# Token mixer of a hybrid decoder: late row root at its entry, q, k, v, z pieces as 512- and 256-column products, halves summed on GpSimd

## The chip, the core and the metric

One core of a Trainium2 chip runs the whole kernel. The metric is the device time of one execution in microseconds. An execution uses five engines that run their own instruction queues in order and meet only at semaphores: PE (TensorE, matrix products), ACT (ScalarE), DVE (VectorE), POOL (GpSimd), and SP, which here only issues the loads of weights.

## The reference

Two layers, each FFN, mixer, FFN, on 256 positions of 1024 channels in fp32:

```python
for l in range(DEPTH):                                   # DEPTH = 2
    h = rms_norm(x, ffn1_norm[l])
    x = x + 0.5 * swiglu(h, ffn1_w_gate[l], ffn1_w_up[l], ffn1_w_down[l])   # D_FF = 2816
    h = rms_norm(x, mix_norm[l])
    proj = h @ w_in[l]                                    # 1024 -> 3080 columns
    aq, ak, av, pu, dq, dk, dv, dz, db, da = jnp.split(proj, split_at, axis=-1)
    ...                                                   # rope on aq, ak
    ya = dilated_attention(aq, ak, av).reshape(B, S, ATT_WIDTH)
    yb = multiscale_pool(pu, pool_w[l], pool_scale[l])
    yc = gated_deltanet(dq, dk, dv, dz, db, da, dn_conv_w[l], ...)
    x = x + jnp.concatenate([ya, yb, yc], axis=-1) @ w_out[l]
    h = rms_norm(x, ffn2_norm[l])
    x = x + 0.5 * swiglu(h, ffn2_w_gate[l], ffn2_w_up[l], ffn2_w_down[l])
return rms_norm(x, final_norm)
```

`rms_norm` is `x * rsqrt(mean(x*x) + eps) * w`, with one root for each position (row). In `gated_deltanet`, q, k and v (4 heads of 128) go through a causal convolution of 4 taps and a silu, q and k are normalised, z goes through a silu, and b and a give the gates (a log decay and a beta for each head and position). Then comes the chunked delta rule, which needs a triangular inverse for each head.

## The kernel before

**Products in parts.** All large products are in fp32r, which keeps fewer bits than fp32. So a weight piece (128 x 1024, 512 KB) is split: ACT casts it to a high part `Wh` (L1215) and DVE subtracts to get the low part `Wl` (L1626). The input is split likewise into `Xh` and `Xl`, which lie side by side in `X`. A product is Wh·Xh + Wh·Xl + Wl·Xh. There are six slots for pieces, and SP loads the next piece into a slot when its low cast is done.

**Two forms of a piece.** `wide_piece` (L695 to 704, the FFNs') multiplies `Wh` with `Xh` and `Xl` together, 512 columns, eight times, and then `Wl` with `Xh`, 256 columns, into the right half of the bank, eight times. Somebody must then add the halves. `column_piece` (L685, the mixer's) adds all three products up in the same 256 columns, 24 products of 256 columns each, and leaves nothing to add.

**FFN.** 22 tiles of 128 hidden channels. x is turned raw on PE, and ACT and DVE scale it by the norm weight (a column) while they split it. The root of each row comes in later: PE spreads it over all partitions (L752), DVE copies it as `rB` (L1749), and POOL multiplies it in (L589, L591).

**Mixer.** Its entry is of another form. `norm` finds the roots (ACT L1293 to L1301, DVE L1645 to L1700), POOL and DVE multiply x by the norm weight, `turn_rows` (L681) turns and scales x in one product with a diagonal of roots, and `split_rows` splits it. Then come 17 pieces, i = 0 to 16: 0 to 7 are q and k of four heads, 8 holds the gates' columns, 9 to 12 are v, 13 to 16 are z. Pieces 17 on are attention, pooling and output. For each of q, k, v, ACT takes the first tap straight from the bank (L1392, `conv_first`), DVE the other three (L1809, `conv_rest`), and ACT applies silu (L1397) and, for a pair of q and k, the squares (L1403) that PE sums (L868).

The gates: DVE copies their columns (L1840), PE turns them (L861), DVE runs 16 small steps (L1844 to L1865) with an exp and a ln on ACT between. POOL forms `grow` (L611), PE sums it up over positions (L899), DVE takes differences (L1890), ACT exponentiates them. Gram products (L917), `LT` and `aT` on DVE, a select of POOL (L619, `lt_done`), and DVE's product `DT` (L1917) follow. PE turns `DT` (L930) and ACT copies it to `Dm` (L1471). From there six levels (from L985) double the inverted blocks, with the attention's pieces between.

**What sets the order.** Nothing but the code: every engine's queue is written out by hand. In the mixer ACT's queue is, for i from 0 to 7,

```python
hi_mix(layer, i + 3)
conv_first(i)
if i >= 1:
    conv_silu(i - 1)
    if i % 2 == 0:
        square(i // 2 - 1)
```

and DVE's is

```python
lo_mix(layer, i + 3)
conv_rest(i)
```

`hi_mix` waits for the slot's load and for the product that used its high part last; `lo_mix` waits for the `hi_mix` of the same piece.

## Time and profile before

| | us |
|---|---|
| median of 3 runs | 1103.63 (1102.22 to 1105.7) |
| the profiled execution, its own time | 1107.22 |
| its span in the trace | 1105.4 |
| PE busy | 1066.8 (97%) |
| DVE busy | 726.8 (66%) |
| ACT busy | 609.7 (55%) |
| POOL busy | 213.9 (19%) |

The profile is of one execution. Its span begins with the first instruction and ends with the last; 1.8 us of its time lie outside it. Products overlap in PE's pipeline and their ends are modelled, so a length of 0.39 us says little about pace; the distance of two starts does. "Idle before" names what ended an engine's wait. The mixers lie at about 207 to 371 and 746 to 910 us, the FFNs between and around them.

### The profile page before, as it was taken

The numbers are of one execution on the slowest core, as the hardware profiler recorded it, in microseconds if no ns is written. First come the engines' busy times: TensorE is split into PE (matmuls) and PEld (weight loads), VectorE is DVE, ScalarE is ACT, GpSimd is POOL, SyncE is SP. The second block draws the span as 40 slices with busy tenths as digits, with TensorE's granted clock in tenths as the row PEclk, the third lists the DMA queues.
The fourth block names the chain that finished last, engine by engine and source line by source line (L and its number), as shares of the span: only waits on it lengthen the run. The fifth ranks groups of instructions, "written<-read, shape, count | busy, mean of one in ns | idle before, by whom it ended". The sixth has DMA issues, their size and how long they took to land.

```text
span 1105.4 us, 18284 instructions
## 1 busy us (share of the span) xinstructions
PE 1066.8 (97%) x6179; PEld 929.7 (84%) x6179; DVE 726.8 (66%) x1125; ACT 609.7 (55%) x1057; POOL 213.9 (19%) x255
## 2 busy tenths in 40 slices
PE   6899999899999999999999999998999999999996
PEld 5788888798997788888878888888899878888885
DVE  4666666688437676666677666667773667666665
ACT  5555555567445655555565555556653556555554
POOL 1312112571020131211222112120002002211212
PEclk9899999999999999999999999999999999999999
DMA  6866667364321476666647666674352044766661
GB/s 198 271 186 194 189 183 216 100 168 115 119 73 39 137 240 188 195 188 185 195 133 213 190 183 196 189 202 121 100 152 96 21 152 152 210 189 184 196 191 39
DMA packets 252151, 179.27 MB, mean 162 GB/s; under 512 B 5891, under 2 KB 237576, under 8 KB 251976
## 3 DMA queue, kind: packets, MB, share of 16 engines
q1 hardware_dynamic: 251168, 176.71, 54.3%
q0 software_dynamic: 336, 1.71, 0.4%
q8 instruction: 30, 0.49, 0.2%
q10 hardware_dynamic: 600, 0.22, 0.1%
q14 instruction: 17, 0.14, 0.0%
HBM read 177.57 MB, written 1.05 MB: 162 GB/s over the span
## 4 chain that ended last, share of the span: by engine, by line
PE 87%; DVE 5%; ACT 4%; DMA 2%; issue 1%; POOL 0%; ACTq 0%; DVEq 0%; POOLq 0%; SPq 0%
PE bank L700 27%; PE bank L703 14%; PE bank L666 12%; PE bank L667 11%; PE bank L668 11%; PE bank L985 2%; PE bank L1009 2%; DMA raw<-in_ffn_w_up 1%; DVE Wl L1626 1%; ACT Wh L1215 1%; PE bank L681 1%; DVE X L1672 1%; PE bank L992 1%; ACT big L1248 1%; PE bank L917 1%
## 5 line engine op out<-in xcount | busy, mean ns | idle before, releaser
L1626 DVE TENSOR_TENSOR Wl<-raw,Wh 128x1024 fp32r<-128x1024 f32 x330 | 417.9, 1273 | 131.6 <-ACT Wh L1215 131.3
L1215 ACT ACTIVATE Wh<-raw 128x1024 fp32r<-128x1024 f32 x330 | 337.6, 1053 | 80.6 <-PE bank L668 74.7
L700 PE MATMUL bank<-X,Wh 128*128 128x512 f32 x1344 | 334.8, 391 | 0.0
L700 PEld LDWEIGHTS bank<-X,Wh 128*128 128x128 f32 x1344 | 247.0, 189 | 47.4
L589 POOL TENSOR_TENSOR gact<-gact,pooled 128x256 f32<-128x256 f32 x88 | 77.5, 880 | 606.5 <-DVE gact L1717 464.2
L703 PEld LDWEIGHTS bank<-X,Wl 128*128 128x128 f32 x1344 | 183.2, 191 | 13.8 <-DVE Wl L1626 1.0
L703 PE MATMUL bank<-X,Wl 128*128 128x256 f32 x1344 | 187.8, 283 | 0.0
L666 PE MATMUL bank<-Wh,aH 128*128 128x512 f32 x352 | 140.0, 398 | 6.4 <-DVE aL L1738 6.0
L667 PE MATMUL bank<-Wl,aH 128*128 128x512 f32 x352 | 138.9, 395 | 0.0
L668 PE MATMUL bank<-Wh,aL 128*128 128x512 f32 x352 | 137.9, 392 | 0.0
L1314 ACT ACTIVATE dec<-bank 128x256 f32<-128x256 f32 x88 | 33.6, 382 | 126.1 <-PE bank L703 125.3
L1331 ACT ACTIVATE aH<-hid 128x256 fp32r<-128x256 f32 x88 | 36.8, 418 | 92.8 <-DVE hid L1732 92.8
L666 PEld LDWEIGHTS bank<-Wh,aH 128*128 128x128 f32 x352 | 67.0, 190 | 20.1 <-issue 8.7
L591 POOL TENSOR_TENSOR gact<-gact,pooled 128x256 f32<-128x256 f32 x88 | 66.3, 754 | 80.8 <-ACT gact L1319 80.8
L666 PE MATMUL bank<-X,Wh 128*128 128x256 f32 x272 | 79.8, 294 | 1.8 <-DVE Wl L1626 1.8
L668 PEld LDWEIGHTS bank<-Wh,aL 128*128 128x128 f32 x352 | 66.7, 190 | 14.7
L1717 DVE TENSOR_TENSOR gact<-bank,dec 128x256 f32<-128x256 f32 x88 | 37.3, 424 | 61.1 <-ACT dec L1314 61.1
L668 PE MATMUL bank<-X,Wl 128*128 128x256 f32 x272 | 77.1, 283 | 0.0
L667 PE MATMUL bank<-X,Wh 128*128 128x256 f32 x272 | 77.1, 283 | 0.0
L667 PEld LDWEIGHTS bank<-Wl,aH 128*128 128x128 f32 x352 | 67.1, 191 | 10.6
L1725 DVE TENSOR_TENSOR hid<-bank,dec 128x256 f32<-128x256 f32 x88 | 37.4, 425 | 47.5 <-ACT dec L1325 47.5
L1738 DVE TENSOR_TENSOR aL<-hid,aH 128x256 fp32r<-128x256 f32 x88 | 37.4, 425 | 42.6 <-ACT aH L1331 42.6
(246 smaller groups left out, 1276.5 us busy)
## 6 DMA issues: line engine op xcount, KB each, us to landing
raw<-in_ffn_w_gate SPq DMA_DIRECT2D x88, 512.0 KB, 4.1
raw<-in_ffn_w_up SPq DMA_DIRECT2D x88, 512.0 KB, 3.7
raw<-in_ffn_w_down SPq DMA_DIRECT2D x88, 512.0 KB, 4.5
raw<-in_w_in SPq DMA_DIRECT2D x50, 512.0 KB, 3.9
raw<-in_w_out SPq DMA_DIRECT2D x16, 512.0 KB, 3.5
cst<-in_consts POOLq DMA_DIRECT2D x1, 1536.0 KB, 9.4
xr<-in_x SPq DMA_DIRECT2D x2, 512.0 KB, 4.5
norm_w<-in_mix_norm SPq DMA_DIRECT2D x2, 512.0 KB, 6.1
```

What stands on the lines that cost most here:

```text
L589: nc.gpsimd.tensor_tensor(gact[:, par, :], gact[:, par, :], rB, ALU.mult).then_inc(gate_scaled.sem, 1)
L591: nc.gpsimd.tensor_tensor(gact[:, par, :], gact[:, par, :], rB, ALU.mult).then_inc(silu_scaled.sem, 1)
L666: nc.tensor.matmul(outp, lh, rh, start=start, stop=False)
L667: nc.tensor.matmul(outp, lh, rl, start=False, stop=False)
L668: return nc.tensor.matmul(outp, ll, rh, start=False, stop=stop)
L700: nc.tensor.matmul(b[:, :], piece(Wh, s)[:, k, :], X[:, k, :, :], start=k == 0, stop=False)
L703: m = nc.tensor.matmul(b[:, SEQ:], piece(Wl, s)[:, k, :], Xh[:, k, :], start=False, stop=k == KT - 1)
L1215: return nc.scalar.activation(Wh[:, s, :], raw[:, s, :], ACT.Copy).then_inc(hi_cast.sem, 1)
L1626: return nc.vector.tensor_tensor(Wl[:, s, :], raw[:, s, :], Wh[:, s, :].bitcast(F32), ALU.subtract).then_inc(lo_cast.sem, 1)
L1717: nc.vector.tensor_tensor(gact[:, par, :], gbank[par][:, 0:SEQ], low[:, 0, par, :], ALU.add).then_inc(gsum_done.sem, 1)
L1725: nc.vector.tensor_tensor(hid[:, par, :], ubank[par][:, 0:SEQ], low[:, 1, par, :], ALU.add).then_inc(usum_done.sem, 1)
L1738: nc.vector.tensor_tensor(aL[:, par, :], hid[:, par, :], aH[:, par, :].bitcast(F32), ALU.subtract).then_inc(al_done.sem, 1)
```

## The change

The mixer's entry takes the FFNs' form (`enter`, `enter_mixer`): raw x is turned into banks 4 to 7, split with `mix_norm` as a column, and the root comes later. The first two pieces are computed in halves as the input becomes ready. For attention and pooling, ACT multiplies the root in as it copies (`scale=stat[:, c, 7:8]`); for the gates, DVE does as it copies.

The q, k, v and z pieces become wide pieces. ACT copies each whole bank (512 columns) into a ring of four places in SBUF, which lie in `PM` and `Dm`; POOL adds the halves and multiplies by `rB`; then come the taps, or z's silu, now with the ring as source. A place is free for copy i when the taps of piece i−4 are done. `PM` and `Dm` are also what the levels use. The tables for rope, which POOL computes once in layer 0, come after the second select. At the kernel's start x is turned before the norm weights, and ACT's squares come first.

```diff
+        def ring(i):
+            t, at = (PM, Dm)[i % 4 // 2], 4 * (i % 2)
+            return t[:, at:at + 4, :].rearrange("p a t -> p (a t)")
...
 # POOL
-                weigh_rows(layer, 1)
-                if layer == 0:
-                    trig_tables()
+                def scale(i):
+                    pool.wait_ge(*evacuated.at(layer, i + 1))
+                    r = ring(i)
+                    nc.gpsimd.tensor_tensor(r[:, 0:SEQ], r[:, 0:SEQ], r[:, SEQ:], ALU.add).then_inc(summed.sem, 1)
+                    pool.wait_ge(*summed.at(layer, i + 1))
+                    nc.gpsimd.tensor_tensor(r[:, 0:SEQ], r[:, 0:SEQ], rB, ALU.mult).then_inc(scaled.sem, 1)
+                pool.wait_ge(*rb_done.at(layer, 2))
+                for i in range(11):
+                    scale(i)
                 pool.wait_ge(*gstep.at(layer, 16))
                 nc.gpsimd.tensor_tensor(grow[:, :, :], tri.unsqueeze(1).broadcast_to([P, UNITS, P]),
...
+                for i in range(11, 14):
+                    scale(i)
                 for c in range(HALVES):
+                    if c == 1:
+                        scale(14)
+                        scale(15)
                     pool.wait_ge(*lt_raw.at(layer, 2 * c + 2))
...
+                if layer == 0:
+                    trig_tables()
 # PE
-                for i in range(8):
-                    split(i)
-                    column_piece(bank[i][:, 0:SEQ], MIX_SLOTS[i],
-                                 inputs_of(layer, 1) if i == 0 else None).then_inc(proj.sem, 1)
+                enter_mixer(layer)
+                for i in range(2, 8):
+                    if i == 4:
+                        pe.wait_ge(*rb_done.at(layer, 2))
+                    wide_piece(bank[i], MIX_SLOTS[i], layer, MIX_BASE + i).then_inc(proj.sem, 1)
                 split(8)
-                pe.wait_ge(*convd.at(layer, 1))
+                pe.wait_ge(*evacuated.at(layer, 1))
                 column_piece(bank[0][:, 0:SEQ], MIX_SLOTS[8]).then_inc(gates_proj.sem, 1)
                 for h in range(2):
-                    split(9 + h)
-                    pe.wait_ge(*convd.at(layer, 2 + h))
-                    column_piece(bank[1 + h][:, 0:SEQ], MIX_SLOTS[9 + h]).then_inc(proj.sem, 1)
+                    pe.wait_ge(*evacuated.at(layer, 2 + h))
+                    wide_piece(bank[1 + h], MIX_SLOTS[9 + h], layer, MIX_BASE + 9 + h).then_inc(proj.sem, 1)
                     if h == 0:
                         pe.wait_ge(*gates_copied.at(layer, 1))
...
 # ACT
+                def evacuate(i):
+                    act.wait_ge(*proj.at(layer, i + 1))
+                    if i >= 4:
+                        act.wait_ge(*convd.at(layer, i - 3))
+                    nc.scalar.activation(ring(i), pieces[i][:, :], ACT.Copy).then_inc(evacuated.sem, 1)
...
-                for i in range(8):
+                evacuate(0)
+                evacuate(1)
+                hi_mix(layer, 4)
+                conv_first(0)
+                for i in range(2, 8):
                     hi_mix(layer, i + 3)
-                    conv_first(i)
-                    if i >= 1:
-                        conv_silu(i - 1)
-                        if i % 2 == 0:
-                            square(i // 2 - 1)
+                    evacuate(i)
+                    conv_first(i - 1)
+                    conv_silu(i - 2)
+                    if i % 2 == 1:
+                        square(i // 2 - 1)
                 hi_mix(layer, 11)
+                conv_first(7)
+                conv_silu(6)
+                evacuate(8)
                 conv_silu(7)
+                square(3)
+                hi_mix(layer, 12)
                 conv_first(8)
-                hi_mix(layer, 12)
-                conv_first(9)
-                square(3)
+                evacuate(9)
...
                     if h == 1:
-                        conv_first(10)
+                        evacuate(10)
...
                 for i in (17, 18, 19):
                     hi_mix(layer, i)
+                evacuate(14)
+                evacuate(15)
                 z_silu(2)
                 z_silu(3)
                 act.preload_act_table_set(LN_EXP)
                 for c in range(HALVES):
                     act.wait_ge(*d0_turned.at(layer, c + 1))
+                    if c == 0:
+                        act.wait_ge(*z_act.at(layer, 4))
...
 # DVE
-                for i in range(8):
-                    lo_mix(layer, i + 3)
+                lo_mix(layer, 3)
+                take_root(layer, 1)
+                lo_mix(layer, 4)
+                for i in range(6):
+                    lo_mix(layer, i + 5)
                     conv_rest(i)
                 lo_mix(layer, 11)
+                conv_rest(6)
                 dve.wait_ge(*gates_proj.at(layer, 1))
-                nc.vector.tensor_copy(gate_cols, bank[0][:, 0:SEQ]).then_inc(gates_copied.sem, 1)
+                dve.wait_ge(*rb_done.at(layer, 2))
+                nc.vector.tensor_tensor(gate_cols, bank[0][:, 0:SEQ], rB, ALU.mult).then_inc(gates_copied.sem, 1)
+                conv_rest(7)
+                lo_mix(layer, 12)
                 conv_rest(8)
-                lo_mix(layer, 12)
```

How the queues stand at three places. The first pair is ACT's queue at the pieces 3 and 4 of q and k. `Wh<-raw` is a high cast, `QK<-bank` or `QK<-PM` a first tap, `QK<-QK` a silu, `early<-QK` a square. Before:

```order
L1215 ACTIVATE Wh<-raw 128x1024 [waits downs_done,landed5]
L1392 ACTIVATE QK<-bank2,prm 128x256 [waits proj]
L1397 ACTIVATE QK<-QK 128x256 [waits convd]
L1403 ACTIVATE early<-QK 128x512 [waits conv_act]
L1215 ACTIVATE Wh<-raw 128x1024 [waits proj,landed0]
```

Now, where `Dm<-bank` is the copy into the ring:

```order
L1245 ACTIVATE Wh<-raw 128x1024 [waits downs_done,landed5]
L1415 ACTIVATE Dm<-bank2 128x512 [waits proj]
L1424 ACTIVATE QK<-PM,prm 128x256 [waits scaled]
L1429 ACTIVATE QK<-QK 128x256 [waits convd]
L1245 ACTIVATE Wh<-raw 128x1024 [waits proj,landed0]
```

The cast into slot 5 (piece 5) was followed by the tap of piece 2 and the silu of piece 1; it is now followed by the copy of piece 2, the tap of piece 1 and the silu of piece 0.

The second pair is DVE's queue at the gates. `gact<-bank0` is the copy of their columns, `ga<-bank0` the first small step, `QK` and `VT` rows are taps. Before:

```order
L1626 TENSOR_TENSOR Wl<-raw,Wh 128x1024 [waits hi_cast]
L1840 COPY gact<-bank0 128x256 [waits gates_proj]
L1809 SCALAR_TENSOR_TENSOR VT<-bank1,prm,VT 128x255 [waits conv1]
L1809 SCALAR_TENSOR_TENSOR VT<-bank1,prm,VT 128x254 [waits conv_mid]
L1809 SCALAR_TENSOR_TENSOR VT<-bank1,prm,VT 128x253 [waits conv_mid]
L1626 TENSOR_TENSOR Wl<-raw,Wh 128x1024 [waits hi_cast]
L1844 COPY ga<-bank0 128x16 [waits gates_in]
```

Now:

```order
L1672 TENSOR_TENSOR Wl<-raw,Wh 128x1024 [waits hi_cast]
L1854 SCALAR_TENSOR_TENSOR QK<-Dm,prm,QK 128x255 [waits conv1]
L1854 SCALAR_TENSOR_TENSOR QK<-Dm,prm,QK 128x254 [waits conv_mid]
L1854 SCALAR_TENSOR_TENSOR QK<-Dm,prm,QK 128x253 [waits conv_mid]
L1890 TENSOR_TENSOR gact<-bank0,pooled 128x256 [waits rb_done,gates_proj]
```

The taps of piece 6 moved between the low cast of piece 11 and the gates' copy, and those of piece 7 came behind it.

The third pair is POOL's queue from `grow` to the selects in layer 0. Before:

```order
L579 TENSOR_TENSOR pooled<-pooled,qT 128x256 [waits trig_step]
L580 TENSOR_TENSOR trig<-pooled,qT 128x256 [waits trig_step]
L611 TENSOR_TENSOR grow<-cst,ga 128x1024 [waits gstep,trig_step]
L619 AFFINE_SELECT LT<-LT 128x512 [waits lt_raw] x2
L631 TENSOR_TENSOR qkr<-big,trig 128x512 [waits att_read]
```

Now (`Dm<-Dm` is a sum of halves, `Dm<-Dm,pooled` its scaling by `rB`):

```order
L615 TENSOR_TENSOR Dm<-Dm,pooled 128x256 [waits summed]
L621 TENSOR_TENSOR grow<-cst,ga 128x1024 [waits gstep]
...
L634 AFFINE_SELECT LT<-LT 128x512
L613 TENSOR_TENSOR Dm<-Dm 128x256 [waits evacuated]
L615 TENSOR_TENSOR Dm<-Dm,pooled 128x256 [waits summed]
L613 TENSOR_TENSOR Dm<-Dm 128x256 [waits evacuated]
L615 TENSOR_TENSOR Dm<-Dm,pooled 128x256 [waits summed]
L634 AFFINE_SELECT LT<-LT 128x512 [waits lt_raw]
L545 CAST pos_f<-pos_i 128x2 [waits consts_in,pos_in]
```

`grow` stands behind the scaling of the ring's copy 10, the second select behind those of copies 14 and 15 (z's third and fourth pieces), and the tables behind the select. Copies are numbered without the gates' piece: copy 8 is piece 9.

## Rows read from the trace of the kernel before

**Rows 1.** The page, part 4: shares of the chain that ended last, by engine.
```profile
PE 87%; DVE 5%; ACT 4%; DMA 2%; issue 1%; POOL 0%; ACTq 0%; DVEq 0%; POOLq 0%; SPq 0%
```

**Rows 2.** Timeline, PE: start and length in us, line, result and operands, count, [idle before].
```profile
32.72 0.77 PE L666 MATMUL bank<-Wh,aH 128*128 128x512 f32 x1 [4.43 <-DVE aL L1738]
...
201.06 0.40 PE L666 MATMUL bank<-Wh,aH 128*128 128x512 f32 x1
...
209.94 1.16 PE L681 MATMUL bank<-diag,big 128*128 128x128 f32 x8 [2.57 <-DVE diag L1700]
...
215.72 0.37 PE L666 MATMUL bank<-X,Wh 128*128 128x256 f32 x1
...
244.84 0.38 PE L861 MATMUL bank<-cst,gact 128*128 128x128 f32 x2
...
260.17 1.96 PE L899 MATMUL bank<-grow,cst 128*128 128x512 f32 x4
```

**Rows 3.** Timeline, PE, entry of the next layer's first FFN.
```profile
549.42 2.00 PE L700 MATMUL bank<-X,Wh 128*128 128x512 f32 x8
...
552.21 0.40 PE L666 MATMUL bank<-Wh,aH 128*128 128x512 f32 x1
...
567.83 2.10 PE L700 MATMUL bank<-X,Wh 128*128 128x512 f32 x8
```

**Rows 4.** Timeline, ACT, the mixer's pieces in layer 0.
```profile
220.03 1.06 ACT L1215 ACTIVATE Wh<-raw 128x1024 fp32r<-128x1024 f32 x1 [1.18 <-DVE ga L2071]
...
223.87 0.42 ACT L1397 ACTIVATE QK<-QK 128x256 f32<-128x256 f32 x1 [1.11 <-DVE QK L1809]
...
224.20 1.04 ACT L1215 ACTIVATE Wh<-raw 128x1024 fp32r<-128x1024 f32 x1
...
226.53 0.42 ACT L1397 ACTIVATE QK<-QK 128x256 f32<-128x256 f32 x1 [0.93 <-DVE QK L1809]
...
227.52 1.04 ACT L1215 ACTIVATE Wh<-raw 128x1024 fp32r<-128x1024 f32 x1
...
239.96 1.05 ACT L1215 ACTIVATE Wh<-raw 128x1024 fp32r<-128x1024 f32 x1
```

**Rows 5.** Timeline, DVE, the mixer in layer 0.
```profile
221.19 1.22 DVE L1626 TENSOR_TENSOR Wl<-raw,Wh 128x1024 fp32r<-128x1024 f32 x1 [1.20 <-ACT Wh L1215]
...
222.33 1.51 DVE L1809 SCALAR_TENSOR_TENSOR QK<-bank,prm,QK 128x255 f32<-128x255 f32 x3
...
231.81 1.22 DVE L1626 TENSOR_TENSOR Wl<-raw,Wh 128x1024 fp32r<-128x1024 f32 x1
...
243.18 0.42 DVE L1840 COPY gact<-bank 128x256 f32<-128x256 f32 x1
...
248.11 0.17 DVE L1844 COPY ga<-bank 128x16 f32<-128x16 f32 x1
...
265.20 2.16 DVE L1890 SCALAR_TENSOR_TENSOR dec<-bank,ga,cst 128x128 f32<-128x128 f32 x8
```

**Rows 6.** Timeline, POOL, the mixer in layer 0.
```profile
228.16 0.75 POOL L575 TENSOR_TENSOR pooled<-pooled,kT 128x256 f32<-128x256 f32 x1
...
232.08 1.54 POOL L575 TENSOR_TENSOR pooled<-pooled,kT 128x256 f32<-128x256 f32 x1
...
254.01 1.90 POOL L611 TENSOR_TENSOR grow<-cst,ga 128x1024 f32<-128x1024 f32 x1 [9.33 <-DVE ga L1865]
```

**Rows 7.** Timeline, ACT, ahead of the levels.
```profile
277.12 1.08 ACT L1471 ACTIVATE Dm<-bank 128x512 f32<-128x512 f32 x2
```

**Rows 8.** Timeline, PE, first products of the levels.
```profile
277.77 2.05 PE L985 MATMUL bank<-Dm,LT 128*128 128x128 f32 x16 [0.20 <-ACT Dm L1471]
```

**Rows 9.** Timeline, ACT, the kernel's start.
```profile
16.85 0.62 ACT L1248 ACTIVATE big<-xr 128x512 f32<-128x512 f32 x1
```

**Rows 10.** Busy time by stretch: PE, PEld, DVE, ACT, POOL, granted clock, DMA share, GB/s.
```profile
32.00:38.00 6.00, 5.28 (x14) 4.21 (x15) 3.87 (x6) 3.92 (x7) 2.37 (x2) 0.56 1.06 411
208.00:216.00 8.00, 5.71 (x34) 5.52 (x35) 4.90 (x12) 3.04 (x9) 7.11 (x13) 0.79 0.00 0
```

More of the change, by code:

```diff
@@ L1239, in x_ready, with inverse, norm_final, enter @@
                     act.wait_ge(*x_new.at(layer, 4 * n + quarter_no(layer, n, c, b)))
-            def enter_ffn(layer, f, cast=None):
-                n = 2 * f
+            def inverse(layer, n, c):
+                act.wait_ge(*var_done.at(layer, 2 * n + c + 1))
+                nc.scalar.activation(stat[:, c, 3:4], stat[:, c, 2:3], ACT.Ln).then_inc(ln_done.sem, 1)
+                act.wait_ge(*ln_done.at(layer, 2 * n + c + 1))
+                nc.scalar.activation(stat[:, c, 4:5], stat[:, c, 3:4], ACT.Exp, scale=-0.5).then_inc(rs_done.sem, 1)
+            def norm_final():
+                for c in range(HALVES):
+                    for b in range(2):
+                        act.wait_ge(*x_new.at(DEPTH, 2 * c + b + 1))
+                        if c == 1:
+                            act.wait_ge(*ss_done.at(DEPTH, b + 1))
+                        nc.scalar.activation(squares[b], xr[:, c, b * NW:(b + 1) * NW], ACT.Square, scale=D_MODEL ** -0.5,
+                                             accum_out=stat[:, c, b:b + 1]).then_inc(ss_done.sem, 1)
+                    inverse(DEPTH, 0, c)
+            def enter(layer, n):
+                first = layer == 0 and n == 0
                 def square(c, b):
@@ L1253, in split @@
                     if j % 4 >= 2:
-                        act.wait_ge(*xl_done.at(layer, SPLITS[n] + j - 1))
-                    nc.scalar.activation(Xh[:, k, :], xt(k), ACT.Copy,
-                                         scale=nrm_all[:, f, layer, k:k + 1]).then_inc(xh_done.sem, 1)
-                if cast is None:
-                    square(0, 0)
-                    square(1, 0)
-                act.wait_ge(*turned.at(layer, 4 * n + (2 if cast is None else 3)))
-                for j in range(4):
-                    split(j)
-                if cast is None:
+                        act.wait_ge(*xl_done.at(layer, 8 * n + j - 1))
+                    nc.scalar.activation(Xh[:, k, :], xt(n, k), ACT.Copy,
+                                         scale=nrm_all[:, n, layer, k:k + 1]).then_inc(xh_done.sem, 1)
+                square(0, 0)
+                square(1, 0)
+                if first:
                     square(0, 1)
@@ L1268, in enter_ffn @@
                         inverse(layer, n, c)
-                else:
-                    cast(0)
+                    act.wait_ge(zeroed.sem, 2)
+                act.wait_ge(*turned.at(layer, 4 * n + (3 if first else 2)))
+                for j in range(4):
+                    split(j)
+                if first:
+                    hi_first(layer, 0, 0)
+                else:
+                    square(0, 1)
+                    square(1, 1)
+                    for c in range(HALVES):
+                        inverse(layer, n, c)
                 act.wait_ge(*turned.at(layer, 4 * n + 4))
@@ L1615, in _ @@
                     hi_first(layer, 1, j)
-                enter_ffn(layer, 1)
+                enter(layer, 2)
                 ffn(layer, 1, next_casts(layer))
-            norm(DEPTH, 0)
+            norm_final()
         @block.vector
@@ L1802, in conv_rest @@
                 def conv_rest(i):
-                    src = ([bank[b] for b in range(8)] + [bank[1], bank[2], bank[7], bank[0]])[i]
+                    src = ring(i)
                     dst = QK[:, i // 2, i % 2, :] if i < 8 else VT[:, i - 8, :]
```

351 lines of the change are left out of this document (166 added, 185 removed).

## The prediction

> **What bounds the kernel now.** I read the chain that ended last first: PE holds 87% of it, with DVE and ACT at 5% and 4% [rows 1]. Then PE's timeline at the mixer's entry. The last products of the first FFN begin at 201.06; the turned and scaled input passes through L681 from 209.94, and piece 0 of the mixer begins at 215.72 [rows 2]. The chain is a row of small steps there: norms, diagonals, turning, splitting. From then on PE has no gap: its ten pieces of 24 products take 215.72 to 244.84, which is 2.91 us each (three products of 256 columns for each of eight blocks) [rows 2].
> A 512-column product with its 256-column partner costs no less: 16 of them take 549.42 to 552.21, 2.79 us [rows 3]. The means in the page's table (391 and 283 ns) are lengths of overlapping instructions and say nothing of this; starts do. So the wider products save 0.12 us a piece and no more.
> Next I read ACT's and DVE's timelines beside PE's. A cast (1.14 from its start to the next start) and three taps (1.51) take DVE 2.65 us a piece [rows 5], so DVE is nearly as full as PE, and the order of its queue and ACT's decides what happens when either gets more to do.
>
> **What the change removes.** The entry now has the form that the FFNs already have: raw x is turned, split with its norm weight, and the row's root is multiplied in later. Such an entry stands in the trace: from the last products at 552.21 to the next piece after two finished ones at 567.83 is 15.62 us [rows 3]. The old entry plus two pieces is 215.72 − 201.06 + 2 × 2.91 = 20.48 us. Gain: 4.9 us a layer. Fourteen wide pieces more give 1.7 us where PE is the bound.
>
> **What it adds, and where that lies.** Every q, k, v, z piece now goes: PE, an ACT copy of 512 columns out of its bank (0.54 us, two take 1.08 [rows 7]), a GpSimd sum, a GpSimd scaling, ACT's first tap, DVE's other taps. GpSimd's two steps take 0.75 us each when nothing disturbs them, 1.54 when DVE's cast is running [rows 6]. With four ring places, latency alone would be covered. The order is not.
> The order of ACT (first pair of ordered rows) is now cast(i+3), copy(i), first tap(i−1), silu(i−2). DVE's is cast(i+3), then taps(i−2). So silu(i−2) waits for taps that stand behind the low cast of the very piece whose high cast ACT has just made, and the next high cast stands behind that silu. Before, silu(i−1) waited for taps behind a cast from ACT's lap before, and the two engines ran side by side. Now a lap is a closed ring, and its parts are in the trace:
> – ACT cast to DVE cast: 220.03 to 221.19, 1.16 us [rows 4, 5]
> – DVE cast to first tap: 221.19 to 222.33, 1.14 [rows 5]
> – three taps to silu: 222.33 to 223.87, 1.54 [rows 4, 5]
> – silu to the next cast: 223.87 to 224.20, 0.33; with a square 226.53 to 227.52, 0.99 [rows 4]
> That is 4.17 us, or 4.83 every second lap: 27.0 us for the six laps from cast 5 to cast 11, where PE wants a piece every 2.8 us. The taps read the ring in SBUF now, not a bank; the step of 0.48 us could be 0.42 at the least, which takes 0.2 off a lap. I keep 4.5.
>
> **The timetable, on layer 0's clock.** By the FFN's entry, PE is ready for piece 2 at 201.06 + 15.62 = 216.7. From there the path to ACT's cast 5 is, as an estimate from the rows' durations: the rest of four small parameter copies 0.6, DVE's cast 3 1.14, the root's copy 0.45, GpSimd's sum and scaling of piece 0 1.6, held up by cast 4 for 1.1, and ACT's first tap 0.4. That is 222.0. Six laps: cast 11 at 248.5 to 249, against 239.96 before [rows 4]. PE waits first for piece 7 at 232, then for 8 at 237.4; the laps decide from there.
> Gates: DVE's copy of their columns stands behind cast 11 and taps 6 (second pair of ordered rows). 249.7 + 1.14 + 1.43 gives 252.2, against 243.18 [rows 5]. PE, in order, stands at their transposes from 243.6 to 252.7. Behind that wait are piece 10, to 255.9, and the sums of squares; ACT's square(3) waits for the first sum, and cast 12 stands behind it at 257.2. DVE's cast 12 and taps 8 come before the gate steps, which start at 260.9 against 248.11 [rows 5]. ACT's table switch is then hidden and the gate steps end 10.7 late.
> GpSimd: `grow` stands behind scale(10), which needs ACT's copy(10) after two inverse norms, at 266.3. So `grow` starts at 269.0 instead of 254.01 [rows 6]. PE was busy with pieces until 260.17 before [rows 2], so only 10.8 of these 15 us are seen, and the second half of the differences on DVE comes 11.0 late (one half is 1.04 of the row's 2.16 [rows 5]).
> Last, the second GpSimd select stands behind scale(14) and scale(15) (third pair). They need ACT's copies 14 and 15, which stand behind three casts, and ACT's copies into `Dm` wait for the last z silu, since `Dm` is part of the ring. By rows: copies at 285.9 and 286.5, two sums and scalings to 289.8, the select, DVE's product and PE's turn 2.3 together as an estimate, `Dm` at 292.1. The levels start at 293.2 against 277.77 [rows 8]: 15.5 us late with the gain of the entry already taken off. The levels, attention and output pieces have the same instructions as before; their scale by a column of `stat` is free. The trig tables of layer 0 move behind the select, about 35 us of GpSimd (it was through with them 9.33 before 254.01 [rows 6]); they end near 326 to 329 and the second rope is due at about 329, so I cost them nothing, with 2 us as the upper end.
>
> **The clock.** After the 4.43 us that PE waited before 32.72 [rows 2], the granted clock was 0.56 from 32 to 38, that is the 1.2 GHz level most of that time; with 2.57 us idle before 209.94 [rows 2] and small products it was 0.79 from 208 to 216 [rows 10]. The new wait before the gates' transposes is 9 us and the one before the second turn of DT about 6 us. At the low level, piece 10 and the first sum of squares take 2.7 us more on the path, and the turns and first level products 1.7 to 3 more. Both ends are kept: 15.5 a layer if the clock never falls, 21 if it falls both times. I take 18, near the upper end, since both waits are longer than the one in the row.
>
> **Kernel's start.** The squares and roots, which stood on ACT from 16.85 on [rows 9], four squares and their roots, some 3 us, move ahead of the splits into idle time; a third row of norms is loaded. Estimate: −1.5 us once (0 to −3).
>
> **Sum.** 2 × 18 − 1.5 = 34.5 us. Against the profiled execution's own 1107.2 that gives 1141.7; that execution lay 3.6 above the median of 1103.6, so for the median 1138. Own range of this case: 2 × 15 − 3 to 2 × 22, 1131 to 1148.
>
> **Rivals.**
> Faster, 5%: the ring hides everything and the entry decides. It needs ACT to run on past silu(i−2), so the taps would have to be done before ACT gets there; that holds only if DVE's cast and taps took under 1 us together, and they take 2.7. The price if it held: −2 × (4.9 + 1.7) − 1.5 gives 1089. I leave the chance for a slip of mine in reading the order.
> Partly covered, 10%: laps are as long as I say, but what follows has slack that I count as path (square(3) earlier, `grow` covered). Then about 8 us a layer: 1118.
> Lock, 10%: DVE and GpSimd hinder each other more than in the timetable. The rows show GpSimd held up by DVE's cast of two SBUF tensors (1.54 at 232.08, beside the cast at 231.81) and not by taps whose source is a bank (0.75 at 228.16) [rows 5, 6]. The new taps read two SBUF tensors. If each lap loses one GpSimd pair, 1.5 us, on DVE, six laps and two v pieces add 12 us at most a layer, half of it likely: 2 × 6 more gives 1150. The Trainium skill, "SBUF — State Buffer", section "SBUF: two separate sides", says that a DVE instruction with two SBUF inputs and a GpSimd one exclude each other, whoever starts first holding the port to its end. The cast's row agrees with that; no row here has such taps beside GpSimd. By that rule the new taps lock where the old did not, which is this rival.
> "No change" has no mechanism that I can name and lies between the first and second: 2%. The forecast itself has 73%.
>
> **Numbers.** About 0.3% of 1103.6, 3.3 us, is what a measurement of this kernel tells from no change. Faster by more: 5%. Within: 2%. Slower: 93%. Range for 8 in 10: 1118, taking in most of the second rival, to 1150.
>
> **What would show it.** ACT's high casts 5 to 11 at 4.2 and 4.8 us in turn, each silu released by DVE's taps; if they come every 2.8, the ring is not closed and I am wrong altogether. A PE wait of about 9 us before the gates' transposes, with a granted clock under 1 behind it; none means the laps are covered. `grow` behind scale(10) and the second select behind scale(15) by 10 us or more. The FFN-like entry 4.9 us shorter, whatever the total does. Taps clearly over 0.48 us, or GpSimd steps over 2 us, would speak for the lock. Spans of the FFN stages should be unchanged.

## The result, and the profile after

| | before | after |
|---|---|---|
| median of 4 runs, us | 1104.66 (1102.22 to 1106.84) | 1160.97 (1159.38 to 1165.07) |
| profiled execution, its own time | 1107.22 | 1159.72 |
| its span | 1105.4 | 1157.4 |
| PE busy | 97% | 93% |

The changed kernel takes 1.0516 of the time of the one before (95% interval 1.0478 to 1.0554): 56 us more. The forecast was 1138, with 1118 to 1150 as its range. The direction and the places were right; the size was short by 23.

The profiled spans differ by 52.0. The levels start at 303.01 instead of 277.77 [rows 8] in layer 0, 25.2 later, and at 869.25 instead of 816.75 in layer 1, 52.5 later. Counted from the last FFN piece before it (196.58 for 198.26, and 762.56 for 737.38), each mixer loses 27 us ahead of its levels, and nothing else in the program moves by as much as 2 us. PE's timeline in the first mixer of the changed kernel (start, length, line, operation, count, idle before), beside [rows 2, 8]:

```profile
196.58 2.00 PE L700 MATMUL bank<-X,Wh 128*128 128x512 f32 x8
...
214.95 2.09 PE L700 MATMUL bank<-X,Wh 128*128 128x512 f32 x8
...
231.54 2.88 PE L700 MATMUL bank<-X,Wh 128*128 128x512 f32 x8 [2.38 <-ACT Wh L1245]
...
255.54 0.69 PE L895 MATMUL bank<-cst,gact 128*128 128x128 f32 x2 [10.39 <-DVE gact L1890]
255.88 3.76 PE L700 MATMUL bank<-X,Wh 128*128 128x512 f32 x8
...
276.52 3.30 PE L931 MATMUL bank<-grow,cst 128*128 128x512 f32 x4 [1.70 <-POOL grow L621]
...
299.54 1.12 PE L961 MATMUL bank<-cst,DT 128*128 128x128 f32 x4 [4.68 <-DVE DT L1968]
...
303.01 2.60 PE L1016 MATMUL bank<-Dm,LT 128*128 128x128 f32 x16
```

The last piece of the FFN starts at 196.58, piece 2 of the mixer at 214.95, 18.4 later. Before, the same two points are at 198.26 (the row below) and 215.72 + 2 × 2.91 = 221.54 [rows 2], 23.3 apart. That is the entry's gain, 4.9, to the tenth. At the last FFN piece itself the changed kernel is 198.26 − 196.58 = 1.7 earlier; whether the new start earned that is taken up below.

```profile
198.26 2.00 PE L700 MATMUL bank<-X,Wh 128*128 128x512 f32 x8
```

The entry's 9.8 in two layers and this 1.7, 11.5 over the whole run, are then lost more than five times over. ACT's timeline, answering to [rows 4]:

```profile
219.91 1.04 ACT L1245 ACTIVATE Wh<-raw 128x1024 fp32r<-128x1024 f32 x1
...
224.52 0.42 ACT L1429 ACTIVATE QK<-QK 128x256 f32<-128x256 f32 x1 [2.69 <-DVE QK L1854]
224.84 1.05 ACT L1245 ACTIVATE Wh<-raw 128x1024 fp32r<-128x1024 f32 x1
...
230.44 1.04 ACT L1245 ACTIVATE Wh<-raw 128x1024 fp32r<-128x1024 f32 x1
...
251.42 1.04 ACT L1245 ACTIVATE Wh<-raw 128x1024 fp32r<-128x1024 f32 x1
...
261.75 0.63 ACT L1435 ACTIVATE early<-QK 128x512 f32<-128x512 f32 x1 [4.03 <-PE bank L902]
```

The `Wh<-raw` rows are casts 5, 6, 7 and 11: laps of 4.93 and 5.60, and 31.5 us for six of them. Each silu waits 2.7 for DVE's taps: the ring is closed, as forecast, but each lap is 0.76 longer than the forecast's 4.17 and 4.83. DVE and POOL show where that is, first DVE (beside [rows 5]), then POOL (beside [rows 6]):

```profile
225.93 1.23 DVE L1672 TENSOR_TENSOR Wl<-raw,Wh 128x1024 fp32r<-128x1024 f32 x1 [1.44 <-ACT Wh L1245]
227.07 2.36 DVE L1854 SCALAR_TENSOR_TENSOR QK<-PM,prm,QK 128x255 f32<-128x255 f32 x3
...
253.64 1.51 DVE L1854 SCALAR_TENSOR_TENSOR QK<-Dm,prm,QK 128x255 f32<-128x255 f32 x3
```

```profile
226.45 1.29 POOL L613 TENSOR_TENSOR Dm<-Dm 128x256 f32<-128x256 f32 x1 [2.76 <-ACT Dm L1415]
227.82 0.81 POOL L615 TENSOR_TENSOR Dm<-Dm,pooled 128x256 f32<-128x256 f32 x1
...
274.39 2.08 POOL L621 TENSOR_TENSOR grow<-cst,ga 128x1024 f32<-128x1024 f32 x1
...
298.12 0.64 POOL L634 TENSOR_SCALAR_AFFINE_SELECT LT<-LT 128x512 f32<-128x512 f32 x1
```

Three taps take 2.36 where POOL's sum and scaling lie beside them (226.45 to 228.6), and 1.51 at 253.64, where POOL rests. The sum takes 1.29 instead of 0.75. Grouped by shape, the taps of 255 columns on the ring's half in `PM` (216 to 262 us; line, operation, operands, count, busy time, mean ns, idle before) take 958 ns on average, the one that meets GpSimd's sum:

```profile
L1854 DVE SCALAR_TENSOR_TENSOR QK<-PM,prm,QK 128x255 f32<-128x255 f32 x4 | 3.8, 958 | 0.0
```

The lock (DVE and GpSimd holding each other up) was a rival with 10% in the forecast, but it does not replace the ring: it is there in each of the six laps, on top of the ring. This is the rest of the mixer, by what PE waited for over the whole run (total, times, longest):

```profile
PE bank L895 <- DVE gact L1890: 19.7, 2, 10.4
PE bank L961 <- DVE DT L1968: 11.7, 4, 4.7
PE bank L700 <- ACT Wh L1245: 6.0, 3, 2.4
...
PE bank L931 <- POOL grow L621: 3.4, 2, 1.7
PE bank L700 <- ACT early L1440: 3.1, 2, 1.6
```

And the clock behind the 10.4 us wait (stretch, length, PE, PEld, DVE, ACT, POOL busy, granted clock, DMA share, GB/s):

```profile
245.00:262.00 17.00, 6.61 (x24) 4.97 (x23) 8.50 (x13) 6.20 (x12) 3.68 (x4) 0.70 0.21 59
```

Piece 10 takes 4.75, from 255.88 to the first sum of squares at 260.63, where a wide piece takes 2.79 at the full clock [rows 3].

### The profile page after: what moved, and what is told of

Its sections match the earlier page's. It is cut to its first block, busy times and chain, and to the rows that moved or that the text cites. A ratio compares the mean times of both kernels' runs of the same rounds, so it can differ in the third digit from the quotient of the medians.

```text
span 1157.4 us, 17864 instructions
## 1 busy us (share of the span) xinstructions
PE 1079.1 (93%) x5899; PEld 923.1 (80%) x5899; DVE 745.5 (64%) x1137; ACT 630.7 (54%) x1097; POOL 266.4 (23%) x313
## 4 chain that ended last, share of the span: by engine, by line
PE 77%; DVE 12%; ACT 6%; issue 2%; POOL 1%; DMA 1%; SPq 0%; DVEq 0%; ACTq 0%; POOLq 0%
PE bank L700 27%; PE bank L703 14%; PE bank L684 9%; PE bank L685 9%; PE bank L686 9%; DVE Wl L1672 3%; ACT Wh L1245 2%; DVE QK L1854 2%; PE bank L1016 2%; PE bank L1040 2%; DVE VT L1854 1%; DVE X L1716 1%; ACT X L1303 1%; PE bank L745 1%; DVE xr L1843 1%
## 5 line engine op out<-in xcount | busy, mean ns | idle before, releaser
L700 PE MATMUL bank<-X,Wh 128*128 128x512 f32 x1568 | 400.0, 398 | 9.2 <-ACT Wh L1245 6.0
L700 PEld LDWEIGHTS bank<-X,Wh 128*128 128x128 f32 x1568 | 291.1, 191 | 71.2 <-ACT Wh L1245 5.2
L703 PEld LDWEIGHTS bank<-X,Wl 128*128 128x128 f32 x1568 | 215.3, 192 | 17.6 <-DVE Wl L1672 2.3
L703 PE MATMUL bank<-X,Wl 128*128 128x256 f32 x1568 | 220.7, 284 | 0.1
L685 PEld LDWEIGHTS bank<-Wl,aH 128*128 128x128 f32 x352 | 66.4, 189 | 10.4
L684 PE MATMUL bank<-Wh,X 128*128 128x384 f32 (+2 forms) x160 | 57.4, 358 | 0.0
L686 PE MATMUL bank<-Wh,X 128*128 128x384 f32 (+2 forms) x160 | 55.5, 347 | 0.0
L685 PE MATMUL bank<-Wl,X 128*128 128x384 f32 (+2 forms) x160 | 55.4, 346 | 0.0
```

The lines of the kernel that those rows point to most:

```text
L684: nc.tensor.matmul(outp, lh, rh, start=start, stop=False)
L685: nc.tensor.matmul(outp, lh, rl, start=False, stop=False)
L686: return nc.tensor.matmul(outp, ll, rh, start=False, stop=stop)
L700: nc.tensor.matmul(b[:, :], piece(Wh, s)[:, k, :], X[:, k, :, :], start=k == 0, stop=False)
L703: m = nc.tensor.matmul(b[:, SEQ:], piece(Wl, s)[:, k, :], Xh[:, k, :], start=False, stop=k == KT - 1)
```

## The experiments

Three theories were on the table. The forecast's is an order that closes ACT and DVE into one lap. The rival's is the lock. A third is that what follows the gates is late for reasons of its own. Each run's ratio is to the kernel before in the same series, whose median was 1103.5 to 1105.2.

**GpSimd's work made tiny.**

```diff
-                    nc.gpsimd.tensor_tensor(r[:, 0:SEQ], r[:, 0:SEQ], r[:, SEQ:], ALU.add).then_inc(summed.sem, 1)
+                    nc.gpsimd.tensor_tensor(r[:, 0:8], r[:, 0:8], r[:, SEQ:SEQ + 8], ALU.add).then_inc(summed.sem, 1)
...
-                    nc.gpsimd.tensor_tensor(r[:, 0:SEQ], r[:, 0:SEQ], rB, ALU.mult).then_inc(scaled.sem, 1)
+                    nc.gpsimd.tensor_tensor(r[:, 0:8], r[:, 0:8], rB[:, 0:8], ALU.mult).then_inc(scaled.sem, 1)
```

> GpSimd's sum and scaling of each ring place are done over 8 columns instead of 256 (so most of the sum and of the root is left out of the output); order and semaphores are those of the changed kernel. Theory (lock): the three taps take 2.36 us beside GpSimd's work and 1.51 where it rests, because DVE and GpSimd wait for each other. Then all taps fall to about 1.5, laps from 4.93 and 5.58 to about 4.2 and 4.8, 0.75 times six per layer in the ring, and with the v taps and the k norms (0.42 against 0.96 and more) about 6 to 8 us a layer: 1161 to about 1147. Rival (reading SBUF costs the taps this much by themselves): taps stay at 2.36, laps within 0.1, time 1155 to 1161.

Measured 1132.57 (1130.74 to 1135.35), 28.4 less than the changed kernel, ratio to before 1.0271 (1.0239 to 1.0303). DVE's taps and ACT's casts 5, 6, 7 in its timeline:

```profile
224.35 1.52 DVE L1854 SCALAR_TENSOR_TENSOR QK<-PM,prm,QK 128x255 f32<-128x255 f32 x3
```

```profile
218.04 1.04 ACT L1245 ACTIVATE Wh<-raw 128x1024 fp32r<-128x1024 f32 x1
...
222.13 1.04 ACT L1245 ACTIVATE Wh<-raw 128x1024 fp32r<-128x1024 f32 x1
...
226.88 1.05 ACT L1245 ACTIVATE Wh<-raw 128x1024 fp32r<-128x1024 f32 x1
```

The same taps on the same SBUF ring take 1.52, so reading SBUF costs nothing by itself: GpSimd beside them does. The lock shows from the other side too: a sum over 8 columns takes 0.20 where DVE leaves it alone (217.11) and 0.75 beside the taps (223.74). Laps are 4.09 and 4.75, and the forecast's ring (4.17, 4.83) is met within 0.1. But the time fell by 14 a layer and not by 6 to 8.

Its levels start at 288.33 against 303.01, 14.7 earlier, from the same start (last FFN piece at 196.64 and 196.58). The two traces show where this comes from. Cast 5 is 1.9 earlier (218.04 against 219.91), because the first piece's sum and scaling are short. The six laps give 5.0 more. From cast 11 to DVE's copy ahead of the differences (274.09 against 285.47) it is 4.5, and in this stretch DVE goes through the taps of v and the norms: taps of 2.35 take 1.52 and norm steps of 0.96 take 0.41, while `grow` keeps its length (2.08 and 2.07). The sums and scalings of the last two z places, which stand ahead of the second select, take 0.9 instead of 3.0, 2.1 less. The last 1.3 come between that select and the levels, where PE ran at a granted 0.50 (299 to 303) in the changed kernel and at 0.81 (285 to 289) here. So the lock is 5.0 + 4.5 = 9.5 of the 14.7 in layer 0, and most of the rest is GpSimd's own shorter work, 1.9 and 2.1, and the clock, 1.3.

**The ring opened.**

```diff
                     conv_first(i - 1)
-                    conv_silu(i - 2)
-                    if i % 2 == 1:
-                        square(i // 2 - 1)
+                    if i >= 3:
+                        conv_silu(i - 3)
+                    if i >= 4 and i % 2 == 0:
+                        square(i // 2 - 2)
...
                 conv_first(7)
+                conv_silu(5)
+                square(2)
+                evacuate(8)
                 conv_silu(6)
-                evacuate(8)
```

> ACT's silu of q and k pieces is one lap later (silu of i-3 behind the copy of i), so that it waits for taps of DVE's lap before; all else as in the changed kernel. Theory (closed lap): laps fall from 4.93 and 5.58 to DVE's own work, a cast 1.14 and locked taps 2.36, 3.5 us; cast 11 comes about 10 us earlier in each layer, PE's wait for the gates falls from 10.4 to 3 or less, and 6 to 9 us a layer are left at the levels: 1161 to about 1145. Rival (the two engines are simply full, or the lock alone makes the laps): laps stay over 4.5 and the time within 4 us of 1161.

Measured 1140.56 (1139.53 to 1140.74), 20.4 less, ratio to before 1.0332 (1.0302 to 1.0362). Cast 5 is at 223.14 and cast 11 at 242.27 in its trace: 19.1 for six laps instead of 31.5. PE's wait for the gates is 6.7, not the 3 that was expected, since DVE with locked taps (up to 2.73) is now the slow engine itself.

**The gates' copy earlier.**

```diff
                 for i in range(6):
+                    if i == 5:
...
+                        nc.vector.tensor_tensor(gate_cols, bank[0][:, 0:SEQ], rB,
+                                                ALU.mult).then_inc(gates_copied.sem, 1)
                     lo_mix(layer, i + 5)
                     conv_rest(i)
                 lo_mix(layer, 11)
                 conv_rest(6)
...
-                nc.vector.tensor_tensor(gate_cols, bank[0][:, 0:SEQ], rB, ALU.mult).then_inc(gates_copied.sem, 1)
```

> DVE copies the gates' columns ahead of the low cast of piece 10 instead of behind that of piece 11 and taps 6; all else as in the changed kernel. Theory (place in the queue): PE's wait before the gates' transposes falls from 10.4 us to under 2, piece 10 and the sums of squares run at the full clock, ACT's square(3) no longer waits 4.0 us; 4 to 6 us a layer earlier at the levels: about 1151. Rival (what follows hangs on ACT's laps and not on this wait): PE's wait moves to the next piece or sum and the time stays within 3 us of 1161.

Measured 1150.91 (1149.73 to 1151.68), 10.1 less; 1151 was expected. PE's timeline there:

```profile
246.67 0.44 PE L895 MATMUL bank<-cst,gact 128*128 128x128 f32 x2 [0.75 <-DVE gact L1887]
247.82 2.08 PE L700 MATMUL bank<-X,Wh 128*128 128x512 f32 x8 [0.71 <-ACT Wh L1245]
...
258.55 1.82 PE L902 MATMUL bank<-early,cst 128*128 128x512 f32 x2 [2.10 <-ACT early L1435]
263.08 3.78 PE L700 MATMUL bank<-X,Wh 128*128 128x512 f32 x8 [2.71 <-DVE ga L1897]
```

The wait falls from 10.39 to 0.75 and piece 10's wide products take 2.08 instead of 3.76. Of the 10 us of the wait only 5 a layer reach the end: new waits of 2.1 and 2.7 stand behind it, for ACT's square, which still follows the laps, and for the first of the gate steps, and the slow products come there (3.78 at 263.08).

**The tail's order.**

```diff
 # POOL
-                for i in range(11):
+                for i in range(10):
                     scale(i)
...
-                for i in range(11, 14):
+                for i in range(10, 14):
                     scale(i)
                 for c in range(HALVES):
-                    if c == 1:
-                        scale(14)
-                        scale(15)
...
+                scale(14)
+                scale(15)
 # ACT
+                evacuate(14)
+                evacuate(15)
                 for i in (17, 18, 19):
                     hi_mix(layer, i)
-                evacuate(14)
-                evacuate(15)
```

> GpSimd makes grow ahead of scaling 10 and the second select ahead of scalings 14 and 15, and ACT copies 14 and 15 ahead of its casts 17 to 19; all else as in the changed kernel. Theory (in-order queues at the tail): grow starts about 3 us earlier, the second turn of DT's halves loses its 4.7 us wait; Dm's copies then wait for z's last silu, which comes 3 us earlier: 3 to 5 us a layer: about 1153. Rival (these waits are covered by the chain through the z silus and the differences): under 1.5 us a layer, 1158 to 1161.

Measured 1161.17 (1157.49 to 1162.66), ratio 1.0515 (1.0478 to 1.0552): no gain. The rival was right. In PE's timeline the waits change hands:

```profile
282.72 1.95 PE L702 MATMUL bank<-X,Wl 128*128 128x256 f32 x8 [2.55 <-DVE Wl L1671]
...
295.99 0.66 PE L960 MATMUL bank<-cst,DT 128*128 128x128 f32 x4 [0.48 <-DVE DT L1967]
302.27 3.15 PE L1015 MATMUL bank<-Dm,LT 128*128 128x128 f32 x13 [4.32 <-ACT Dm L1518]
```

The second turn of DT waits 0.48 instead of 4.68, and the levels wait 4.32 for `Dm`, whose copy stands behind z's last silu and a table switch (ACT's load of another function table, 1.28 us). `grow` comes earlier and locks with a low cast instead (2.83 for a cast of 1.23), and a piece waits 2.55 for that.

**All three orders.** The edit is the last three together.

> The opened ring, the gates' early copy and the tail's new order together, on the changed kernel. The gates' copy takes PE's 6.7 us wait out of the opened ring, of which 2 to 4 us a layer should be left at the levels (alone it gave 10 of 1161); the tail gave nothing alone, because Dm's copies then waited for z's last silu. Theory (order and lock, two separate causes): 1130 to 1138, still slower than before the change by 25 us or more, since GpSimd and DVE still hold each other up. Rival (order is the whole cause): all queues are open now, the entry's gain shows, and the time is at or under 1104.

Measured 1134.82 (1131.47 to 1138.27), ratio 1.0265 (1.0239 to 1.0291), 26 less than the changed kernel and inside what was expected. These orders are not the whole cause. The levels still wait 4.31 a layer for `Dm` here.

**Ring open and GpSimd tiny.**

> The opened ring with GpSimd's steps over 8 columns (most of the sum and of the root left out of the output). If closed lap and lock are two causes that add: laps at PE's pace of 2.8 to 3.0 with taps of 1.5, and a time of 1110 to 1122, under both e1 (1133) and the opened ring (1141). If they are one and the same loss (each opens the same path), it stays at 1130 or more.

Measured 1105.92 (1103.4 to 1110.08), ratio to before 1.0015 (0.9999 to 1.0032): 55 less than the changed kernel. Alone the two gave 28.4 and 20.4, in sum 48.8. They are two causes that add, and without them the kernel is back where it was before the change. It came out below the 1110 to 1122 that was expected.

That is not yet the whole loss, though: the entry's 9.8 are in this kernel too and should have put it under the kernel before. They are lost elsewhere. PE waits 6.1 us in this trace for `DT` before its turns, 1.9 for the norms and 1.4 for `grow`, where the kernel before has no such waits.

**The closed lap alone, in the kernel before.**

```diff
                     conv_first(i)
-                    if i >= 1:
-                        conv_silu(i - 1)
-                        if i % 2 == 0:
-                            square(i // 2 - 1)
+                    conv_silu(i)
+                    if i % 2 == 1 and i < 7:
+                        square(i // 2)
                 hi_mix(layer, 11)
-                conv_silu(7)
```

> The kernel before the change, with ACT's silu of q and k pieces one lap earlier only: silu(i) behind the first tap of i, so that it waits for taps behind the low cast of the same lap. No GpSimd work, no new entry. Theory (closed lap): casts 4.2 to 4.8 us apart instead of 2.9, taps still 1.51, PE waits ahead of piece 6 or later, 5 to 9 us a layer: 1104 to about 1114 to 1122. Rival (the order of these instructions is without weight while taps read banks): within 3 us of 1104.

Measured 1132.95 (1132.09 to 1136.87), ratio 1.0268 (1.0243 to 1.0293): 28 slower, from ACT's silus, with the squares behind them, issued one lap earlier. ACT's casts in its timeline:

```profile
222.21 1.04 ACT L1215 ACTIVATE Wh<-raw 128x1024 fp32r<-128x1024 f32 x1
225.97 0.42 ACT L1397 ACTIVATE QK<-QK 128x256 f32<-128x256 f32 x1 [2.36 <-DVE QK L1807]
226.96 1.04 ACT L1215 ACTIVATE Wh<-raw 128x1024 fp32r<-128x1024 f32 x1
```

Laps without a square are 4.08 to 4.17 and those with one 4.75, where nothing disturbs DVE's cast; where it met the trig tables on GpSimd they are 0.3 to 0.4 longer. This is the forecast's mechanism with neither the new entry nor new work for GpSimd, and its price is 14 a layer, where 5 to 9 were expected; in layer 1, where no tables are made, it is 13.9 ahead of the levels. Eight laps are closed there, casts 3 to 11, and not six.

**The root on DVE, no GpSimd step on the pieces.** Each piece is 24 products of 256 columns, as before the change, and ACT makes no copy.

```diff
 # ACT
-                    evacuate(i)
...
 # DVE
+                    nc.vector.tensor_tensor(dst, pieces[i][:, 0:SEQ], rB, ALU.mult).then_inc(scaled.sem, 1)
...
+                for i in range(2, 8):
+                    lo_mix(layer, i + 3)
+                    mul(i)
+                    conv_rest(i - 1)
```

> The new entry with 256-column pieces as before the change (24 products, one bank half, no sum to make), ACT's copies and GpSimd's two steps gone: DVE multiplies a finished bank by the root into the ring (z into its own place) in one instruction of about 0.42 us, silu of piece i-2 behind the first tap of i-1 and behind taps of DVE's lap before. Theory (order and lock are the loss, the entry is a gain): DVE's lap is 1.14 + 0.33 + 1.43 = 2.9, even with PE's 2.9; taps 1.51 throughout since GpSimd rests; the entry's 4.9 us a layer and the start's 1.7 remain, less 1 to 3 us a layer for DVE's multiplications where it is full: 1094 to 1100, faster than before the change. Rival (the new entry itself costs the mixer something): 1104 or more.

Measured 1107.73 (1105.78 to 1109.68), ratio 1.003 (1.0019 to 1.0041): 53 less than the changed kernel, yet 3 slower than before the change and not faster. Its rival was right on the time. The lap is 2.90 as expected. The entry's gain is there too: from the last FFN piece (199.77) to piece 2 (218.25) are 18.5 us, against 23.3 before. PE's waits show where it went:

```profile
PE bank L666 <- DVE Wl L1635: 5.6, 4, 1.6
...
PE bank L1003 <- ACT Dm L1482: 3.9, 2, 2.0
PE bank L882 <- DVE gact L1868: 2.3, 2, 1.3
```

**Its queues mended.** The edit is against the run before.

```diff
 # DVE
-                lo_mix(layer, 11)
                 nc.vector.tensor_tensor(gate_cols, bank[0][:, 0:SEQ], rB, ALU.mult).then_inc(gates_copied.sem, 1)
+                lo_mix(layer, 11)
...
                 conv_rest(8)
+                lo_mix(layer, 13)
...
-                lo_mix(layer, 13)
+                lo_mix(layer, 14)
                 mul(10)
...
-                lo_mix(layer, 14)
+                lo_mix(layer, 15)
                 l2norm(3)
...
 # ACT
                 conv_silu(7)
-                square(3)
                 conv_first(8)
+                hi_mix(layer, 13)
+                square(3)
```

> The kernel with DVE's multiplication and 256-column pieces (1107.7), with its queues mended where its trace shows PE waiting for DVE: the gates' copy ahead of the low cast of piece 11; casts 13 to 16 one place earlier each (13 beside the wait for the first sum of squares, so that 14 no longer stands behind all norms); the first v tap ahead of square(3). Theory (what the entry gains was lost again in these waits: 1.0 for the gates, 1.2 and 1.6 for low casts 13 and 14, each layer): 3 to 5 us a layer, 1098 to 1102, faster than before the change. Rival (DVE is full from its first cast to the levels, so that moving work within it gives nothing): within 2 us of 1107.7.

Measured 1105.07 (1101.27 to 1109.2), ratio 1.0003 (0.9987 to 1.002). The waits for low casts and the gates are gone from its trace (0.3 and 0.2 us), but that for `Dm` grew to 2.2 a layer. 2.7 were gained, not 6 to 10, and nothing against the kernel before.

**z's last silus later.** The edit is against the run before.

```diff
-                z_silu(2)
-                z_silu(3)
-                act.preload_act_table_set(LN_EXP)
...
                     for i in LEVEL_CASTS[n]:
                         hi_mix(layer, i)
+                    if n == 1:
+                        z_silu(2)
+                        z_silu(3)
+                        act.preload_act_table_set(LN_EXP)
```

> As the kernel with mended queues, and z's last two silus with the table switch behind them moved from ahead of Dm's copies to ACT's idle time in the second level. Theory: PE's wait of 2.0 us for Dm ahead of the levels goes: 3 to 4 us less than that kernel, 1095 to 1099. Rival (with Dm early, PE waits for the levels' first masked product or for DVE's casts 17 to 19 instead): within 1 us of it.

Measured 1099.71 (1098.0 to 1101.97), ratio to before 0.9956 (0.994 to 0.9973). This is 5.4 less than the kernel with mended queues and 5.4 less than the kernel before in the same series, 0.4% and small, but clear of the noise. PE's first level products in its two layers, with no wait ahead of them:

```profile
271.37 1.95 PE L1003 MATMUL bank<-Dm,LT 128*128 128x128 f32 x16
...
806.26 1.95 PE L1003 MATMUL bank<-Dm,LT 128*128 128x128 f32 x16
```

Against 277.77 [rows 8] and 816.75 they are 6.4 and 10.5 earlier; 1.5 of that stands before the first mixer, where this trace is ahead (last FFN piece at 196.78 for 198.26), so the first mixer gains 4.9 and the second 4.1. The expectation named a gain of 3 to 4 and a range of 1095 to 1099; the gain is larger, and the median lies 0.7 above the range, which had counted on more from the mended queues.

## Why the prediction was wrong

**The entry: right.** 4.9 us a layer, as written.

**The start: not shown, and its agreement is luck.** The 1.7 at the last FFN piece looks like the 1.5 of the sum. But the first FFN's first output products start later in the changed kernel than at 32.72 before [rows 2]:

```profile
33.00 0.47 PE L684 MATMUL bank<-Wh,aH 128*128 128x512 f32 x1 [3.39 <-DVE aL L1784]
```

What it gains, it gains behind that row, and by the clock: from 30 to 40 us, behind that wait of 3.39, its granted clock was 1.00, and the kernel before had 0.66, behind its wait of 4.43. The run with the closed lap in the kernel before has the old start, and its trace reaches the last FFN piece at 196.73, as early as the changed kernel. The run with the gates' copy earlier has the new start and the low clock where the kernel before had it; its row stands at 31.20, 1.5 earlier, and 0.9 are left at the last FFN piece (197.31). So at this landmark the start is worth 0.2 or 0.9, by which traces are compared, and the 1.5 is not confirmed.

**The closed ring: right as a mechanism.** Silus released by DVE's taps, casts in turn shorter and longer, a PE wait of 10.4 before the gates (9), `grow` behind scaling 10, the second select behind scaling 15. The kernel before with only this order shows the ring without the new entry or new work for GpSimd, and the changed kernel with tiny GpSimd steps has the laps that the rows gave.

**The lap's size: wrong, the step that failed.** The sum took the three taps at 1.54 from a row in which their source was a bank, and for the ring in SBUF allowed only that they might be quicker (0.42 a step). They took 2.36, six laps 31.5 instead of 27.0. The lock stood among the rivals as a thing that might or might not happen, with half of 12 us a layer at a 10% chance. By its own evidence it was a term of the sum: the row in which GpSimd was held up by a cast of two SBUF tensors (1.54 at 232.08) was there [rows 6], the new taps read two SBUF tensors, and GpSimd's two steps fall in every lap. The Trainium skill, "SBUF — State Buffer", section "SBUF: two separate sides", says that a DVE instruction with two SBUF inputs and a GpSimd one that reads SBUF exclude each other. The traces agree with that rule (2.36 beside GpSimd, 1.51 and 1.52 without).

**The lock's place: too narrow.** It was weighed for the ring and two v pieces. It works behind the gates too. Taps of piece 8, forecast at 1.43, take 2.35; the gate steps start at 266.78 instead of 260.9, of which 2.8 came with the gates' lateness. `grow` starts at 274.39 instead of 269.0, and the levels at 303.01 instead of 293.2. With GpSimd's steps tiny, DVE's way from cast 11 to the differences is 4.5 shorter.

**Clock: a little short.** Half of its range, 2.5 of 5.5 us a layer, was in the sum. Piece 10 lost 4.75 − 2.79 = 2.0 (2.7 was written for piece and sum; the sums of squares ran at full speed again). Behind the second wait, from the turn of DT's second half to the levels, 299.54 to 303.01 is 3.5, at a granted 0.50. In the run with tiny GpSimd steps the same stretch is 2.2 (from 286.11, the row below, to 288.33), so at least 1.3 were lost. The two make 3.3 a layer, 0.8 more than the sum had, and that is little of the 9 a layer that were missing.

```profile
286.11 0.66 PE L961 MATMUL bank<-cst,DT 128*128 128x128 f32 x4 [2.61 <-DVE DT L1968]
```

**Terms put at nothing.** The trig tables behind the select and the scale by a column of `stat` were costed at nothing, and cost nothing in the end: from the levels of layer 0 to the last FFN piece before the second mixer is 459.6 in both kernels. The scale is not free on ACT (a copy of 384 columns takes 0.58 with it and took 0.49 without), but PE's way does not show it.

**The sum.** 2 × 18 − 1.5 = 34.5 was forecast and 52.0 came between the spans. 2 × 18 would have had to be 2 × 27. With the lock as a term, at the 9.5 a layer that the run with tiny GpSimd steps shows (5.0 in the laps, 4.5 behind the gates), it would have read 2 × 27.5 − 1.5 = 53.5. This is worked out with hindsight: the rows before the change gave the kind of the loss and not these two lengths.

**"Faster, 5%" was right to be small,** but the entry's gain that it named is real: with the ring open and GpSimd's steps tiny the kernel is where it was before, and with the root on DVE, mended queues and z's last silus out of the way it is 5.4 us under it.

**What stays open.** Why both removals together gain 55 where the parts gain 49; an opened ring gives DVE room that only unlocked taps can use, but that was argued and not tried. And no run has the wide pieces and their sums on GpSimd in an order that keeps the entry's gain.

## What to carry to other kernels

When two in-order engines feed each other, write down for each wait in which lap the thing waited for was issued. If it is the same lap, in both directions, the lap is the sum of both engines' work and their slack no longer counts; ACT's silus issued one lap earlier, with the squares behind them, were worth 28 us in the kernel before. And when an operand moves from a bank to SBUF, or a step to GpSimd, take the duration from a row with the same neighbours, not only the same shape.

A wait that is long in the list may be only the last of several that end together: the tail's 4.7 us went, and 4.3 appeared one instruction later.

## What was not expected of the hardware

With the same instructions at the start, PE's slow stretches in the first 40 us came at other places from one execution to the next. Two kernels with the same start are the changed one and the one with the root on DVE (stretch, length, PE, PEld, DVE, ACT, POOL busy, clock, DMA share, GB/s). First the changed one:

```profile
0.00:20.00 20.00, 10.12 (x35) 8.53 (x36) 8.95 (x21) 13.10 (x26) 0.19 (x4) 1.00 0.80 258
30.00:40.00 10.00, 7.00 (x35) 5.95 (x35) 5.51 (x9) 6.21 (x12) 3.35 (x4) 1.00 1.06 384
```

Then the one with the root on DVE:

```profile
0.00:20.00 20.00, 10.04 (x35) 8.49 (x36) 8.96 (x21) 13.09 (x26) 0.19 (x4) 0.80 0.81 257
30.00:40.00 10.00, 6.62 (x18) 5.12 (x18) 4.92 (x9) 5.61 (x10) 3.84 (x5) 0.66 1.06 387
```

The second puts all that follows 3.2 us later (the first turn of the mixer's input at 207.60 against 204.40). Only 0.6 of that is there at the first FFN piece (24.38 against 23.75); the other 2.6 come from the second slow stretch, behind PE's wait for the first output products. The 3.2 are as much as the whole difference between some of these kernels, so landmarks of two traces are compared only from a point behind their starts. The traces of the opened ring and of all three orders have both slow stretches too.

The granted clock of a short stretch does not tell all. Both traces have four 512-column products at half pace, which the record puts at 1.00 in the first (16 to 20 us) and at 0.50 in the second:

```profile
16.72 2.04 PE L745 MATMUL bank<-X,Wh 128*128 128x512 f32 x4 [0.64 <-ACT Wh L1245]
```

```profile
16.73 2.05 PE L727 MATMUL bank<-X,Wh 128*128 128x512 f32 x4 [0.64 <-ACT Wh L1232]
```

In the run with the gates' copy earlier the same products take 1.16, at 16.62. So the lengths of the products are read beside the clock.
